# Recurrence levels on column quarters: inner levels and diagonal per chunk of 32 tokens in a compact matrix

## The reference, cut to what matters

```
f = lb + (1 - lb) * sigmoid(f_logit);  logf = log(f);  k = 1 - f
b = cumsum(logf)
decay = exp(where(causal, b[t] - b[s], -inf))
att = einsum('tk,sk,tsk->ts', q, k, decay)
o = att @ v   (+ what the state carries over from earlier chunks)
```

## Time and profile before

| | us |
|---|---|
| median of 3 runs | 2050.76 (2048.22 to 2052.22) |
| the profiled execution, its own time | 2052.06 |
| its span in the trace | 2050.3 |
| PE busy | 2018.8 (98%) |
| DVE busy | 1119.0 (55%) |
| ACT busy | 941.5 (46%) |
| POOL busy | 6.4 |
| half clock of PE in the recurrence | two stretches, 1109.8 to 1116.6 and 1130.3 to 1133.7 |

### The profile page before, as it was taken

The page is one execution under the profiler, slowest core; times in us unless marked ns, Lnnn a source line. Parts: engine busy times, 40 slices in busy tenths (PEclk is TensorE's granted clock), DMA queues, the critical chain, the costliest instruction groups (busy, mean ns, idle before and its releaser), DMA issues.

```text
span 2050.3 us, 25732 instructions
## 1 busy us (share of the span) xinstructions
PE 2018.8 (98%) x9814; PEld 1667.8 (81%) x9814; DVE 1119.0 (55%) x1404; ACT 941.5 (46%) x1193; POOL 6.4 (0%) x16
## 2 busy tenths in 40 slices
PE   8999999999999999999998999999999999999998
PEld 6788888888888888877777788888888888888886
DVE  5454545455445555766667775644445454444444
ACT  5444444444454444455553465554444444444443
POOL 0000000000000000000001000000000000000000
PEclk9999999999999999999999999999999999999999
DMA  8666666666656557565442365566666666655554
GB/s 285 188 191 188 187 188 190 188 191 209 213 187 193 187 169 221 176 197 154 133 133 83 123 201 170 155 194 189 190 189 190 190 188 185 213 188 193 194 195 144
DMA packets 198824, 376.44 MB, mean 184 GB/s; under 512 B 13152, under 2 KB 19680, under 8 KB 198624
## 3 DMA queue, kind: packets, MB, share of 16 engines
q1 hardware_dynamic: 195984, 372.97, 59.5%
q10 hardware_dynamic: 2768, 2.48, 0.4%
HBM read 373.31 MB, written 2.10 MB: 183 GB/s over the span
## 4 chain that ended last, share of the span: by engine, by line
PE 96%; DVE 2%; ACT 1%; issue 1%; DMA 1%; SPq 0%; DVEq 0%; ACTq 0%
PE psum L1453 90%; PE psum L1476 2%; PE psum L1655 1%; PE psum L1688 1%; PE psum L1555 1%; PE psum L1465 1%; PE psum L1668 0%; PE psum L1744 0%; DVE kgT L1265 0%; DMA w_raw<-in_w_out 0%; DVE att L1276 0%; DMA w_raw<-in_g 0%; DVE qfT L1263 0%; PE psum L1634 0%; PE psum L1885 0%
## 5 line engine op out<-in xcount | busy, mean ns | idle before, releaser
L895 DVE TENSOR_TENSOR w_lo<-w_raw,w_hi 128x1024 fp32r<-128x1024 f32 x696 | 852.2, 1227 | 889.8 <-ACT w_hi L488 888.1
L488 ACT ACTIVATE w_hi<-w_raw 128x1024 fp32r<-128x1024 f32 x696 | 736.6, 1060 | 1038.5 <-PE psum L1453 1010.5
L1453 PE MATMUL psum<-w_hi,xT_hi 128*128 128x512 f32 (+1 forms) x1824 | 715.7, 392 | 10.9 <-DVE w_lo L895 9.1
L1453 PE MATMUL psum<-w_hi,xT_lo 128*128 128x512 f32 (+1 forms) x1824 | 709.3, 389 | 0.0
L1453 PE MATMUL psum<-w_lo,xT_hi 128*128 128x512 f32 (+1 forms) x1824 | 709.3, 389 | 0.0
L1453 PEld LDWEIGHTS psum<-w_hi,xT_hi 128*128 128x128 f32 x1824 | 343.6, 188 | 86.1 <-issue 16.2
L1453 PEld LDWEIGHTS psum<-w_hi,xT_lo 128*128 128x128 f32 x1824 | 343.6, 188 | 71.2
L1453 PEld LDWEIGHTS psum<-w_lo,xT_hi 128*128 128x128 f32 x1824 | 343.9, 189 | 68.5
L1453 PE MATMUL psum<-w_hi,ffT_hi 128*128 128x512 f32 x784 | 306.3, 391 | 0.0
L1453 PE MATMUL psum<-w_hi,ffT_lo 128*128 128x512 f32 x784 | 305.2, 389 | 0.0
L1453 PE MATMUL psum<-w_lo,ffT_hi 128*128 128x512 f32 x784 | 305.0, 389 | 0.0
(11 more groups left out here) (230 smaller groups left out, 868.3 us busy)
## 6 DMA issues: line engine op xcount, KB each, us to landing
w_raw<-in_g SPq DMA_DIRECT2D x176, 512.0 KB, 3.7
w_raw<-in_u SPq DMA_DIRECT2D x176, 512.0 KB, 3.6
w_raw<-in_d SPq DMA_DIRECT2D x176, 512.0 KB, 4.5
w_raw<-in_w_in SPq DMA_DIRECT2D x88, 512.0 KB, 3.7
w_raw<-in_w_out SPq DMA_DIRECT2D x32, 512.0 KB, 3.7
w_raw<-in_cw SPq DMA_DIRECT2D x8, 512.0 KB, 3.8
w_raw<-in_wk SPq DMA_DIRECT2D x8, 512.0 KB, 5.2
w_raw<-in_wq SPq DMA_DIRECT2D x8, 512.0 KB, 3.6
```

What stands on the lines that cost most here:

```text
L488: nc.scalar.activation(w_hi[:, slot], w_raw[:, slot], ACT.Copy).then_inc(w_hi_ready, 1)
L895: nc.vector.tensor_tensor(w_lo[:, slot], w_raw[:, slot], w_hi[:, slot].bitcast(F32), ALU.subtract)\
L1453: mm = nc.tensor.matmul(dst[:, t, 0:width], act_t, w[:, slot, kk, 0:width], start=(first and kk == 0 and n == 0), stop=(last and kk == KT_ ...
```

## The change

CB = 32 and N_IN = 5: the levels 1, 2, 4, 8, 16 (the inner ones) and the diagonal are computed per chunk of 32 tokens.

- PE: each inner level makes four matmuls per head and tile in place of two, each with 32 stationary and 16 moving columns, whose outputs lie in the four quarters of the PSUM partitions. The diagonal makes four of 32 x 32 in place of one of 128 x 128. Level 32 makes two of 32 stationary and 32 moving columns. Level 64 is as before.
- DVE: diagonal and inner levels go into a compact att_c (128 partitions x 8 heads x 2 tiles x 32). The diagonal is two multiplications of 128 x 256 in place of four of 128 x 512. An inner half level is one COPY_PREDICATED of 128 x 128 in place of two of 64 x 256. Level 32 has no copy on DVE any more. The masks shrink from 128 x 448 to 128 x 112 (with a small identity), and the cast to 128 x 80.
- ACT: for each half it spreads att_c into att with four copies of 32 partitions x 256, and takes level 32 out of PSUM with two copies of 32 x 256, besides its copy of level 64.
- POOL: three memsets put zeros into the part of att below the diagonal blocks.
- Waits: the matmuls between the tiles wait for `lv_top` 2 in place of `lv_taken`; those with the values wait for `lv_top` 4, `att_spread` 2 and `att_zeroed` 3.

```
 ACT, recurrence_step
-                elif k >= 15:
+                elif k >= 3 + 2 * N_IN:
                     n, half = k - 3, (k - 3) % 2
-                    act.wait_ge(dg_taken, 4)
+                    hs = slice(4 * half, 4 * half + 4)
+                    m = LEVELS[n // 2]
+                    if m == CB:
+                        act.wait_ge(lv_taken, 2 * N_IN - 1 + half)
+                        for j in range(P // CB):
+                            rows = slice(CB * j, CB * j + CB)
+                            last = nc.scalar.activation(att[rows, hs, :, rows]..., att_c[rows, hs]..., ACT.Copy)
+                        last.then_inc(att_spread, 1)
                     act.wait_ge(lv_done, n + 1)
+                    for s in range(P // (2 * m)):
+                        ... one copy of psum to att per block of 2m tokens
+                    last.then_inc(lv_top, 1)
 DVE, recurrence_step
-                    for b in range(4):
-                        dve.wait_ge(dg_done, b + 1)
-                        ... att 128x512 = psum * ident
+                    dve.wait_ge(mask_loaded, 16)
                     for half in range(2):
+                        dve.wait_ge(dg_done, half + 1)
+                        ... att_c 128x256 = psum * ident_c
                         nc.vector.tensor_tensor(qfT[:, hs], qfT[:, hs], fT[:, hs], ALU.mult).then_inc(qk_ready, 1)
...
+                if l >= N_IN:
+                    return
                 if l:
                     dve.wait_ge(lv_taken, n - 1)
-                if m == P // 2:
-                    return
-                for s in range(2):
-                    ... copy_predicated 64x256
-                last.then_inc(lv_taken, 1)
+                else:
+                    dve.wait_ge(dg_taken, half + 1)
+                ... one copy_predicated 128x128 into att_c
 POOL, at its end
+            pool.wait_ge(hq_turned, 2)
+            pool.wait_ge(tot_ready, 2 * len(LEVELS) - 2)
+            for i, (r0, r1, c0, c1) in enumerate(((CB, 2 * CB, 0, CB), (3 * CB, P, 2 * CB, 3 * CB), (2 * CB, P, 0, 2 * CB))):
+                if i:
+                    pool.wait_ge(att_zeroed, i)
+                nc.gpsimd.memset(att[r0:r1, :, :, c0:c1]..., 0.0).then_inc(att_zeroed, 1)
 PE, recurrence_step
-                          kgT[:, h, ts], qfT[:, h, ts]  (128 x 128 per head and tile)
+                for j in range(P // CB):
+                    matmul(psum[j * CB:(j + 1) * CB, 4 + b // 2, c0:c0 + CB],
+                           kgT[:, h, r0:r0 + CB], qfT[:, h, r0:r0 + CB])
...
-                        for s in range(2):
-                            ... psum[64 * s:64 * s + 64], 32 moving columns
+                        if m < CB:
+                            for j in range(P // CB):
+                                ... psum[32 * j:32 * j + 32], 16 moving columns
 PE, after the levels
-            pe.wait_ge(lv_taken, 2 * len(LEVELS) - 2)
+            pe.wait_ge(lv_top, 2)
...
-            pe.wait_ge(lv_top, 2)
+            pe.wait_ge(lv_top, 4)
+            pe.wait_ge(att_spread, 2)
+            pe.wait_ge(att_zeroed, 3)
```

More of the change, by code:

```diff
@@ L116 @@
 LEVELS = [1, 2, 4, 8, 16, 32, 64]
+CB = 32
+N_IN = 5
 def layer_program(nc, a, c, out):
@@ L746, in recurrence_step @@
                     last.then_inc(g_silu, 1)
[L747 removed]
+                elif k >= 3 + 2 * N_IN:
                     n, half = k - 3, (k - 3) % 2
[L749 to L753 removed]
+                    hs = slice(4 * half, 4 * half + 4)
[4 more added lines that the diff above has]
+                            rows = slice(CB * j, CB * j + CB)
+                            last = nc.scalar.activation(att[rows, hs, :, rows].rearrange("p h t s -> p (h t) s"),
+                                                        att_c[rows, hs].rearrange("p h t s -> p (h t) s"), ACT.Copy)
+                        last.then_inc(att_spread, 1)
+                    act.wait_ge(lv_done, n + 1)
+                    for s in range(P // (2 * m)):
+                        r0 = 2 * m * s
+                        last = nc.scalar.activation(att[r0:r0 + m, hs, :, r0 + m:r0 + 2 * m].rearrange("p h t s -> p (h t) s"),
+                                                    psum[r0:r0 + m, 4 + n % 4, 0:8 * m].rearrange("p (c s) -> p c s", s=m),
+                                                    ACT.Copy)
+                    last.then_inc(lv_top, 1)
             out_at = [0]
@@ L1720, in recurrence_step @@
                             for t in range(NT):
-                                h, ts = 2 * b + hh, slice(t * P, (t + 1) * P)
-                                mm = nc.tensor.matmul(psum[:, 4 + b, (2 * hh + t) * P:(2 * hh + t + 1) * P],
-                                                      kgT[:, h, ts], qfT[:, h, ts], start=True, stop=True)
-                        mm.then_inc(dg_done, 1)
+                                for j in range(P // CB):
+                                    h, r0 = 2 * b + hh, t * P + j * CB
+                                    c0 = (2 * (h % 4) + t) * CB
+                                    mm = nc.tensor.matmul(psum[j * CB:(j + 1) * CB, 4 + b // 2, c0:c0 + CB],
+                                                          kgT[:, h, r0:r0 + CB], qfT[:, h, r0:r0 + CB],
+                                                          start=True, stop=True)
+                        if b % 2:
+                            mm.then_inc(dg_done, 1)
                     return
@@ L1924, in constants @@
     causal = np.where(key[None, :] <= tok[:, None] + P, 0.0, NEG)
-    masks = np.zeros((P, len(LEVELS), P // 2), np.float32)
-    for l, m in enumerate(LEVELS):
-        late = (np.arange(P // (2 * m))[:, None] * 2 * m + m + np.arange(m)[None, :]).ravel()
-        hit = (tok[:, None] // (2 * m) == late[None, :] // (2 * m)) & (tok[:, None] % (2 * m) < m)
-        masks[:, l, :] = hit
+    masks = np.zeros((P, N_IN * CB // 2 + CB), np.float32)
+    row = tok % CB
+    for l, m in enumerate(LEVELS[:N_IN]):
+        late = (np.arange(CB // (2 * m))[:, None] * 2 * m + m + np.arange(m)[None, :]).ravel()
+        hit = (row[:, None] // (2 * m) == late[None, :] // (2 * m)) & (row[:, None] % (2 * m) < m)
+        masks[:, l * CB // 2:(l + 1) * CB // 2] = hit
+    masks[:, N_IN * CB // 2:] = row[:, None] == np.arange(CB)[None, :]
     blk = (tok[:, None] // N_CMP == np.arange(REP)[None, :]).astype(np.float32)
```

54 lines of the change are left out of this document (29 added, 25 removed).

## The result

The changed kernel takes 2036.97 us (median of 5, 2034.58 to 2040.29) against 2048.3 us of the kernel before on the same chip; the ratio is 0.9945, 95% interval 0.9935 to 0.9956. The kernel before, measured again later, came out at 2048.1 to 2048.6; the 2050.76 on which the forecast rests was the median of three runs, and single runs of it lie mostly near 2048 and in part between 2050.5 and 2052.7.

What follows compares the result with a forecast made beforehand. PE was taken to bound the kernel, and DVE's queue its recurrence stage; 11.1 us gained less 2.5 for the clock gave 8.6, so 2052.1 became 2043.5, and 1.3 less for the median 2042.3 us; range 2039 to 2048.4.

Steps and rivals of the forecast that it cites:

- Bound and mechanism: PE bounds the whole kernel, but the recurrence stage lasts as long as DVE's queue, 41.0 us, 12.8 of it masked copies.
- The base: Starting time: the profiled execution of 2052.1 us, with the median shown 1.3 us below it.
- DVE's price: Masked copies in DVE's queue fall from 12.8 to 3.6 us, 9.2 us saved, with bounds of 7.3 and 10.0.
- The start of DVE's queue: At the diagonal, fewer and smaller multiplications let DVE reach the residual addition at 1098.6 instead of 1100.8, 2.2 us earlier.
- Both queues together: PE's and DVE's queues end at 1129.0 and 1130.4; matmuls between the tiles start at 1130.7, 11.1 us earlier.
- PE's record: Each small matmul record in the stage costs 18 ns, so an inner half level takes 1.2 us and the diagonal 2.35.
- Rival 1: PE's records get no cheaper, 29 to 32 ns; gain 3 us less one for the clock, 2048.5 us; 22%.
- the floor in between: PE's records in the stage cost 22 to 25 ns each, giving 2045.5 us; 15%.
- Clock: PE's clock falls to half once or twice in the stage, partly absorbed, costing 2.5 us of the gain.
- Signs: Right if inner bursts take 1.2 to 1.4 us, copies 0.44 and 0.30, and PE is busy over 9 of 10 us.
- ACT, POOL, the mask load: ACT's new copies (4.4 us, bound 7.1), POOL's memsets (under 5 us) and the smaller mask load cost nothing.
- Rival 4: PE runs the stage from about 1105 at half clock, 17 us lost against a gain of 11, 2056 us; 6%.

Runs made afterwards that it cites:

- e2_split_copies: Changed kernel with each inner masked copy cut into two of 64 partitions x 128; 2039.24 us, ratio 0.9949 to the kernel before.
- e6_no_compact: Changed kernel without the compact matrix: DVE writes straight into att in pieces of 32 partitions, ACT spreads nothing; 2050.89 us, ratio 1.0010 to the kernel before.
- e1_pe_twice: Changed kernel with every inner-level matmul made twice, 128 records in a burst in place of 64; 2055.85 us, ratio 1.0033 to the kernel before.
- e7_both: Changed kernel with DVE's second residual addition moved behind the levels and extra matmuls in PE's waits for kgT; 2036.84 us, ratio 0.9940 to the kernel before.

## Why the prediction was wrong, by its own steps

- **Bound and mechanism: right.** The stage was nearly as long as DVE's queue (PE's last fill ended 0.5 us after DVE's last kgT), the gain came from the masked copies, and it stayed to the end. In the stage 12.7 us were won, and the medians differ by 11.3.
- **The base: wrong by 2.5 us.** The forecast rests on 2050.76. The same kernel measured again gives 2048.1 to 2048.6, and 2048.3 less the forecast gain of 8.5 would be 2039.8, inside the range. The profiled execution (2052.06) was longer still, and part of the cause is in its trace: two stretches at half clock outside the stage, which the changed kernel's profile does not have (kernel before, then changed kernel; the clock is the third number from the end):

```profile
901.60:905.00 3.40, 3.40 (x13) 2.78 (x12) 2.71 (x8) 0.77 (x2) 0.00 (x0) 0.50 0.54 154
```
```profile
901.60:905.00 3.40, 3.40 (x17) 2.81 (x16) 3.12 (x11) 1.46 (x2) 0.00 (x0) 1.00 0.00 0
```

  The diagonal starts 4.0 us earlier in the changed kernel's profile, though ahead of it only the mask load was changed. Whether such stretches also make the other long runs long is not shown; the kernel before has one trace.
- **DVE's price, the step that failed.** "Saved: 12.8 - 3.6 = 9.2 us", with bounds of 7.3 and 10.0, took the copies at their durations. These were right (0.44 and 0.30 forecast, 0.44 and 0.29 measured). What counts in a queue is the time to the next instruction. Before, a pair of copies held the queue for 1.5 us at m = 1 and 2 and for 0.9 above, in most half levels with 0.12 us more behind kgT; a whole one now holds it for 0.2. That is about 4 x 1.4 + 6 x 0.8 + 2 x 1.0 = 12.4 us off the queue, outside the bounds. e2_split_copies and e6_no_compact show the same price from the other side.
- **The start of DVE's queue: too small by 0.8.** From the first record of the diagonal to the residual addition it took 7.1 us before and takes 4.1 now, 3.0 us less where 2.2 were forecast. DVE could start 0.9 us into the diagonal, not 1.35, because PE's records were cheaper than the 18 ns taken.
- **Both queues together: half right.** DVE waited for PE for 2.2 us in the stage and for 0.3 before (the queue that was read as "without a gap" had that one), so 1.9 us came back; the sum had nothing for it, and the walk 0.85 us at half level 8. Of the 2.2, 0.6 lie behind the fill at half clock and 1.1 behind the next one, which it and the pause of PE pushed back; the pause was not in the list. The parts measured give 3.0 + 12.4 - 1.9 - 0.4 (PE's last fill) = 13.1 us against 12.7 of stage; 0.4 us are not accounted for.
- **PE's record: wrong.** 18 ns were forecast, 9 measured between records of a burst. The mistake was to scale the pair of two halves; the spacing within one quarter is, by estimate, some 32 to 35 ns and four quarters share it. The floor near 25 ns of "TensorE: Matmul & The Clock Gate" (section "Wait — 56ns, not 53.3ns?") and the overhead of about 60 cycles of "TensorEngine Tiling (Array Packing)" (section Instruction Overhead), both of the Trainium skill, do not show between records of different quarters, which stand 9 ns apart. Rival 1 and the floor in between are refuted as stated. (Redone with the prediction's own terms, 25 ns a record gives 40.5 us and a gain of 7.6, not 6.5.) A limit of another kind exists: 22 ns a record once several hundred follow each other (e1_pe_twice).
- **Clock: a step with too much certainty.** 2.5 us were subtracted for one or two falls. There was one, the fill under it took 4.47 us instead of 2.95, and DVE waited 0.6 us behind it; e7_both without any fall was no shorter. Without this term the forecast gain is 11.1 us, and 11.3 was measured. That agreement is luck: the copies and the start were too small by 3.2 and 0.8, the waits too small by 1.9, and 1.4 us of the profiled stage do not appear in the medians.
- **Signs.** Bursts took 0.74 us and not 1.2 to 1.4, and PE was busy for 87% of the stage and not for over 90%; the prices of the copies came as announced.
- **ACT, POOL, the mask load: right**, at nothing.
- **Rival 4 (slower, by the clock)** did not happen. e1_pe_twice came out slower, by 0.33%, with 64 records more in each burst, but there pauses and falls of the clock came together, and no run divides them.

## What to carry to other kernels

Price an instruction in a busy queue by the start of the next one, not by its duration, and read that from the order of time. In this kernel it paid to give up two or four DVE instructions, each on its own part of the partitions, for one on all 128, even at the price of a compact layout that an idle engine must spread. When matmuls are cut into more and smaller ones, count the instructions too: they may fit in a burst and still be asked for faster than they are brought.

## What the runs showed of the hardware that was not expected

- Where the multiplications of the levels and the copies all start at partition 0, the next one starts before the end of the one ahead; copies that alternate between first partitions (0 and 64, or 0, 32, 64 and 96) wait for the end of the one before. COPY_PREDICATED, duration and time to the next start: 128 x 128 0.29 and 0.20 us (0.44 and 0.22 at m = 1, 2), 128 x 256 0.43 and 0.33 (0.73 and 0.51), 64 x 256 0.435 and 0.44 (0.725 and 0.73), a pair of 64 x 128 0.61 and 0.65 (0.90 and 0.94). A first copy of 128, 64 or 32 partitions started 0.60 us after the kgT multiplication ahead of it where DVE's last read of PSUM had started at partition 0 too, and 0.71 to 0.72 us after it where that read had started at another. No run changes the first partition alone.
- Instructions of PE come in blocks of about 0.016 MB (52 of them 0.85 MB in the changed kernel), about 256 instructions each by the differences between four kernels. The pauses lie 128 or 256 records, 256 or 512 instructions, apart, and end 2.2 to 2.8 us after the start of a block. In twelve places PE stood still for 1.5 to 2.65 us this way, and half levels of DVE behind it waited as well.
- fp32 matmuls with 32 stationary columns stand 16 ns apart over two quarters of the array's columns and 9 ns over four, so by estimate some 32 to 35 ns within one quarter, with 16 or 32 moving columns alike (the diagonal: 128 records in 1.32 us).
